# A sequence block on one core: the state-space mixer's y products two head pairs at a time, a group's sum of squares one step later

## What is computed

```python
a_cum = jnp.cumsum(a_dt, axis=-1)
xdt = x * dt[..., None]
seg = a_cum[..., :, None] - a_cum[..., None, :]
decay = jnp.exp(jnp.where(causal, seg, -jnp.inf))
cb = jnp.einsum('bclgn,bcsgn->bcgls', cm, bm)
y_diag = jnp.einsum('bcgls,bcgels,bcsgep->bclgep', cb, decay, xdt)
...
y = y + d_skip * xs
y = y.reshape(b, l, D_INNER) * jax.nn.silu(z)
y = grouped_rmsnorm(y, norm_g)
return y @ w_out
```

## Time and profile before

| what | value |
|---|---|
| median of 3 runs | 918.33 us (917.94 to 918.78) |
| profiled execution, its own time | 918.76 us |
| span in its profile | 917.0 us |
| TensorE busy | 908.1 us (99%) |
| VectorE busy | 618.6 us (67%) |
| ScalarE busy | 508.9 us (55%) |
| GpSimd busy | 37.3 us (4%) |
| chain that ended last | TensorE 96%, VectorE 2%, ScalarE 1%, DMA 1% |
| granted TensorE clock | 0.996 of full speed over the span |

### The profile page before, as it was taken

One profiled execution on the slowest core, in us unless ns is written; L12 is line 12 of the kernel. 1 busy time (PEld: TensorE's weight loads), 2 busy tenths in 40 slices (PEclk: granted clock), 3 DMA queues, 4 the chain that ended last, 5 costly groups with the idle time before them and its releaser, 6 DMA issues.

```text
span 917.0 us, 14456 instructions
## 1 busy us (share of the span) xinstructions
PE 908.1 (99%) x5920; PEld 817.0 (89%) x5920; DVE 618.6 (67%) x777; ACT 508.9 (55%) x762; POOL 37.3 (4%) x52
## 2 busy tenths in 40 slices
PE   9999999999999999999999999999999999999997
PEld 7999998888899898888888999988998898888885
DVE  7888477895764677777744846766855667777533
ACT  6565488874755574444433855666755645444333
POOL 1000011120000000000000220000000000000000
PEclk9999999999999999999999999999999999999999
DMA  9855554235552566555555697433651565555551
GB/s 283 272 183 181 161 167 133 94 106 194 184 207 92 157 209 194 195 185 183 184 186 199 224 256 238 138 139 113 212 181 46 186 205 184 185 190 189 201 197 46
DMA packets 120986, 162.27 MB, mean 177 GB/s; under 512 B 4109, under 2 KB 106965, under 8 KB 120934
## 3 DMA queue, kind: packets, MB, share of 16 engines
q1 hardware_dynamic: 117828, 151.47, 50.3%
q0 software_dynamic: 3104, 10.06, 3.5%
q10 hardware_dynamic: 2, 0.00, 0.0%
HBM read 160.45 MB, written 1.07 MB: 176 GB/s over the span
## 4 chain that ended last, share of the span: by engine, by line
PE 96%; DVE 2%; ACT 1%; DMA 1%; issue 0%; DVEq 0%
PE bank L476 25%; PE bank L548 16%; PE bank L563 9%; PE bank L554 8%; PE bank L489 8%; PE bank L496 8%; PE bank L502 8%; PE bank L628 2%; PE bank L930 2%; PE bank L901 2%; PE bank L693 1%; PE bank L820 1%; PE bank L733 1%; PE bank L1067 1%; PE bank L859 1%; PE bank L850 1%
## 5 line engine op out<-in xcount | busy, mean ns | idle before, releaser
L1501 DVE TENSOR_TENSOR w_lo<-w_raw,w_hi 128x2048 fp32r<-128x2048 f32 x134 | 306.0, 2288 | 128.9 <-ACT w_hi L1099 128.4
L1099 ACT ACTIVATE w_hi<-w_raw 128x2048 fp32r<-128x2048 f32 x134 | 256.0, 1915 | 194.3 <-DMA w_raw<-in_ffn_w_gu_dram 92.5
L548 PE MATMUL bank<-actT,w_hi 128*128 128x512 f32 x640 | 152.9, 391 | 0.0
L548 PEld LDWEIGHTS bank<-actT,w_hi 128*128 128x128 f32 x640 | 117.6, 188 | 23.0 <-issue 0.2
L554 PEld LDWEIGHTS bank<-actT,w_lo 128*128 128x128 f32 x640 | 82.1, 191 | 3.1
L554 PE MATMUL bank<-actT,w_lo 128*128 128x256 f32 x640 | 83.0, 283 | 0.0
L489 PE MATMUL bank<-actT,w_hi 128*128 128x256 f32 x560 | 74.2, 285 | 0.0
L496 PE MATMUL bank<-actT,w_hi 128*128 128x256 f32 x560 | 72.9, 283 | 0.0
L502 PE MATMUL bank<-actT,w_lo 128*128 128x256 f32 x560 | 72.9, 283 | 0.0
L489 PEld LDWEIGHTS bank<-actT,w_hi 128*128 128x128 f32 x560 | 69.6, 191 | 1.2 <-issue 0.8
L496 PEld LDWEIGHTS bank<-actT,w_hi 128*128 128x128 f32 x560 | 69.7, 192 | 0.0
(11 more groups left out here) (252 smaller groups left out, 1337.9 us busy)
## 6 DMA issues: line engine op xcount, KB each, us to landing
w_raw<-in_ffn_w_gu_dram SPq DMA_DIRECT2D x44, 1024.0 KB, 5.1
w_raw<-in_ffn_w_down_dram SPq DMA_DIRECT2D x22, 1024.0 KB, 4.9
w_raw<-in_ssm_w_in_dram SPq DMA_DIRECT2D x20, 1024.0 KB, 5.4
w_raw<-in_mem_w_kv_dram SPq DMA_DIRECT2D x16, 1024.0 KB, 5.4
w_raw<-in_ssm_w_out_dram SPq DMA_DIRECT2D x8, 1024.0 KB, 5.0
w_raw<-in_mem_w_q_dram SPq DMA_DIRECT2D x8, 1024.0 KB, 6.1
w_raw<-in_mem_w_o_dram SPq DMA_DIRECT2D x8, 1024.0 KB, 5.0
w_raw<-in_w_kv_dram SPq DMA_DIRECT2D x8, 1024.0 KB, 5.5
```

What stands on the lines that cost most here:

```text
L548: pe.matmul(bank[:, b + c, :], hi[:, slot, cols], actT[:, k].rearrange("p e n -> p (e n)"), start=k == 0, stop=False, skip_group_check=True)
L1099: act.activation(hi[:, u % SLOTS, :], raw[:, u % SLOTS, :], ACT.Copy).then_inc(w_hi_done, 1)
L1501: dve.tensor_tensor(lo[:, s, :], raw[:, s, :], hi[:, s, :].bitcast(F32), ALU.subtract).then_inc(w_lo_done, 1)
```

## The change

The y products are made for two pairs at every second step: pairs 0 and 1 in step 3, 2 and 3 in step 5, up to 14 and 15 in step 17. VectorE takes both pairs in the same step (14 and 15 still by its entry for step 16). `xtok` and `mt` get a fourth place, and ScalarE's wait for a free place looks back four pairs. The sum of squares of a group moves one step later on TensorE, and with it 1/rms, the rounded half and the remainder of the first three groups; the last group's stay. The squares on ScalarE stay where they are in each step.

```diff
--- before.py
+++ after.py
@@ -92,9 +92,11 @@
         NAME_OF.append((_name, _i))
 NUNITS = len(NAME_OF)
 
-Y_TAKEN = {p + LAG: (p,) for p in range(XT - 2)}
-Y_TAKEN[XT] = (XT - 2, XT - 1)
-Y_REST = {8: 0, 12: 1, 18: 2, 20: 3}
+Y_MADE = {p + LAG + 1: (p, p + 1) for p in range(0, XT, 2)}
+Y_TAKEN = {**Y_MADE, XT: (XT - 2, XT - 1)}
+del Y_TAKEN[XT + 1]
+Y_REST = {9: 0, 13: 1, 18: 2, 20: 3}
+RS_STEPS = {6: 0, 10: 1, 14: 2, 17: 3}
 SSD_SPLITS, SSD_COPIES = {}, {}
 for _n, (_name, _i) in enumerate(SSD_FILL_UNITS):
     _step = fill_step(6 * _n)
@@ -245,9 +247,9 @@
 
 
         conv_acc, o = shared("conv_acc", [P, 2, 2, S], F32, 0)
-        xtok, o = shared("xtok", [P, 3, ST, P], F32, 0)
+        xtok, o = shared("xtok", [P, 4, ST, P], F32, 0)
         at_mt = o
-        mt, o = shared("mt", [P, 3, 2, CAUS], F32, o)
+        mt, o = shared("mt", [P, 4, 2, CAUS], F32, o)
         first_row, _ = shared("first_row", [P, D], F32, 0)
         ones_row, _ = shared("ones_row", [P, P], F32, 4096)
         cum_rest, o1 = shared("cum_rest", [P, S], F32, at_mt + 2048)
@@ -817,9 +819,9 @@
                     pe.wait_ge(y_ready, j - 1)
                 for e in range(2):
                     rows = slice(e * HD, (e + 1) * HD)
-                    pe.matmul(bank[rows, 3 + j % 2 * 3, 0:S], xtok[:, j % 3, 0, rows], mt[:, j % 3, e, 0:S],
+                    pe.matmul(bank[rows, 3 + j % 2 * 3, 0:S], xtok[:, j % 4, 0, rows], mt[:, j % 4, e, 0:S],
                               start=True, stop=False, skip_group_check=True)
-                    ins = pe.matmul(bank[rows, 3 + j % 2 * 3, P:S], xtok[:, j % 3, 1, rows], mt[:, j % 3, e, S:CAUS],
+                    ins = pe.matmul(bank[rows, 3 + j % 2 * 3, P:S], xtok[:, j % 4, 1, rows], mt[:, j % 4, e, S:CAUS],
                                     start=False, stop=True, skip_group_check=True)
                 ins.then_inc(y_mm, 1)
 
@@ -864,13 +866,13 @@
                         ssd_cb(g + 1)
                 if j < XT:
                     fill_piece(2 * j + 1)
-                if LAG <= j < XT + LAG:
-                    ssd_y(j - LAG)
+                for pair in Y_MADE.get(j, ()):
+                    ssd_y(pair)
                 if j >= XT:
                     fill_piece(2 * j)
                     fill_piece(2 * j + 1)
-                if j > LAG + 1 and (j - LAG - 2) % GT == GT - 1:
-                    ssd_ssq((j - LAG - 2) // GT)
+                if j > LAG + 2 and (j - LAG - 3) % GT == GT - 1:
+                    ssd_ssq((j - LAG - 3) // GT)
 
             def w_out_ready(i):
 
@@ -1315,27 +1317,27 @@
                 if j < XT:
                     g = j // GT
                     act.wait_ge(xtok_mm, j + 1)
-                    act.activation(xtok[:, j % 3], bank[:, 7, 0:S].rearrange("p (t n) -> p t n", n=P), ACT.Copy).then_inc(xtok_ready, 1)
-                    if j >= 3:
-                        act.wait_ge(y_mm, j - 2)
+                    act.activation(xtok[:, j % 4], bank[:, 7, 0:S].rearrange("p (t n) -> p t n", n=P), ACT.Copy).then_inc(xtok_ready, 1)
+                    if j >= 4:
+                        act.wait_ge(y_mm, j - 3)
                     for h in (2 * j, 2 * j + 1):
 
                         act.wait_ge(row_mm, h + 1)
-                        row, decay = bank[:, 4 + h % 2, :], mt[:, j % 3, h % 2, :]
+                        row, decay = bank[:, 4 + h % 2, :], mt[:, j % 4, h % 2, :]
                         act.activation(decay[:, 0:S], row[:, 0:S], ACT.Exp, bias=dtc[:, 7, 0, h:h + 1])
                         act.activation(decay[:, S:CAUS], row[:, S:CAUS], ACT.Exp, bias=dtc[:, 7, 1, h:h + 1]).then_inc(decay_ready, 1)
                     if j % GT == CB_STEP and g + 1 < SSM_GROUPS:
                         copy_cb(g + 1)
                 if c == XT + 1:
                     hi_upto(U[("w_out", 3)])
-                if c > 1 and c % GT == 1:
-
-                    act.wait_ge(ssq_mm, c // GT)
+                if c in RS_STEPS:
+
+                    act.wait_ge(ssq_mm, RS_STEPS[c] + 1)
                     own.mark(act.activation(rs[:, 0, :], bank[:, 2, 0:S], ACT.Ln, bias=eps_col, scale=1.0 / (GT * P)))
                     own.wait()
                     act.activation(rs[:, 1, :], rs[:, 0, :], ACT.Exp, scale=-0.5).then_inc(rs_ready, 1)
-                if c > 2 and c % GT == 2:
-                    g = c // GT - 1
+                if c - 1 in RS_STEPS:
+                    g = RS_STEPS[c - 1]
                     act.wait_ge(yn_ready, g + 1)
                     act.activation(y_hi[:, g * GT:(g + 1) * GT, :], z[:, g * GT:(g + 1) * GT, :], ACT.Copy).then_inc(y_hi_done, 1)
                 if 0 < c <= XT:
@@ -1771,7 +1773,7 @@
                     if j % GT == 0:
                         dve.wait_ge(cb_causal, g + 1)
                     dve.wait_ge(decay_ready, 2 * j + 2)
-                    dve.scalar_tensor_tensor(out=mt[:, j % 3], in0=mt[:, j % 3], scalar=BIG,
+                    dve.scalar_tensor_tensor(out=mt[:, j % 4], in0=mt[:, j % 4], scalar=BIG,
                                              in1=cbT[:, g % 2:g % 2 + 1, :].broadcast_to([P, 2, CAUS]),
                                              op0=ALU.min, op1=ALU.mult).then_inc(mt_ready, 1)
                     if j % GT == CB_STEP + 1 and g + 1 < SSM_GROUPS:
@@ -1785,8 +1787,8 @@
                     dve.tensor_tensor(z[:, pair, :], z[:, pair, :], xbc[:, pair, :], ALU.mult).then_inc(y_ready, 1)
                 if c == XT + 1:
                     lo_upto(U[("w_out", 3)])
-                if c > 1 and c % GT == 1:
-                    g = c // GT - 1
+                if c in RS_STEPS:
+                    g = RS_STEPS[c]
                     dve.wait_ge(rs_ready, g + 1)
                     dve.wait_ge(y_ready, GT * (g + 1))
                     for k in range(g * GT, (g + 1) * GT):
```

## The result

The changed kernel takes **922.09 us** (median of 6 runs, 921.33 to 924.37), the kernel before, run beside it, 918.67 us (6 runs, 917.94 to 920.88). The ratio is **1.0033**, with a 95% interval of 1.0019 to 1.0047: slower by 3.4 us. The forecast was +2.7 us (921.0, range 918.9 to 922.8). The profiled execution took 922.07 us, its span is 920.3 us, against 918.76 and 917.0 before.

The account below looks back on a forecast made before the run. TensorE, busy 99%, bounds the kernel; the moved wait makes ScalarE and VectorE the bound from step 3. +2.2 up to step 15's transposes, +0.25 behind them and +0.25 queue growth give +2.7 on 918.33: 921.0 us, range 918.9 to 922.8.

Parts of the forecast that it names:

- Sign, place and mechanism: Odd steps: even pair's square waits for VectorE's product, holding up the bank 7 copy TensorE's transposes need; kernel slower.
- TensorE's own saving: Y products in eight double visits: 2.4 us from the cheaper second pair plus 0.2 from the sums, 2.6 in all.
- The start of the chain: Step 3: exponentials, then VectorE's operations on the first even pair; its square on ScalarE starts at 149.45 us.
- The loop: ScalarE and VectorE from one even square to the next, two steps each; five of them, steps 3 to 13, 39.36 us.
- From the last even square to T15: Square, cast, copy and hand-off up to the transposes of step 15: 0.30, 0.95, 0.38 and 0.1 us.
- Behind T15: After step 15's transposes: two double visits, 3.2 us, instead of three single ones, 2.85; with cheaper change-overs +0.25 us.
- the forecast's queue growth: ScalarE's operations recorded longer in a full queue: five loops of 0.05 us, +0.25.
- Moving rs, y_hi and y_lo one step costs nothing by itself: VectorE and ScalarE work after the group sums: no cost, since only the projection and the next group's sum want it.
- The saving: Rival: ScalarE keeps ahead of TensorE's transposes and the 2.6 us are gained, 915.7 us; chance 0.07.
- The shorter loop: Rival: the ScalarE and VectorE two-step loop is shorter than summed, 917.5 to 920.1 us, say 919.5; chance 0.16.
- GpSimd's additions: Rival: additions of squares slow VectorE's chain, five loops losing 0.5 us each, 923.5 us; chance 0.08.
- The second pair at its full 0.95: Rival: second pair in a TensorE visit costs a whole visit, 921.6 us; counted with the forecast, together 0.69.

Follow-up runs that it names:

- e1: Changed kernel with the squares of both pairs made together, one step behind their products: 917.65 us, ratio 0.9992 to the kernel before.
- e2: Kernel before, single visits kept, with only each even pair's square moved into the step that makes its product: 925.23 us, ratio 1.0061.
- e8: Changed kernel with squares paired one step behind their products, and the second group's y remainder in step 16 instead of 13: 917.02 us, ratio 0.998.
- e3: Changed kernel with GpSimd adding only 1 of the 256 columns of each square: 922.93 us, ratio 1.004 to the kernel before.
- e4: Kernel before with only the group sum, 1/rms, rounded half and remainder one step later, y products still single: 919.24 us, ratio 1.0004.
- e7: Changed kernel with the group sum, 1/rms, rounded half and remainder back in their old steps: 925.7 us, ratio 1.0065 to the kernel before.

## Why the prediction was right, and where it was off

- **Sign, place and mechanism were right.** The forecast was a wait of ScalarE at the even pair's square in every odd step, some 13 us in all, and behind it TensorE at its door, some 5 us over about five steps. Measured: 14.0 us, and 6.0 us in five waits (5.6 by the steps of e1). e1 takes the wait away and with it the loss; e2 makes it in the kernel before, with its loss.
- **TensorE's own saving: 2.6 forecast.** The second pair was taken at 0.65 and costs 0.69; the double visit was forecast as about 1.5 and costs 1.64. The loop of e8, in which no wait is left, gives the whole: 2.22. So the term was 0.4 too large. Eight times 2 x 0.95 - 1.64 is 2.1, not 2.4. The 0.65 came from the scores, read as 4.01 - 3.41 = 0.60; but the step of 3.41 begins behind a visit and that of 4.01 does not, so they cost 0.66. The sums give the rest, 0.1 to 0.15: a sum costs 0.49 before (two steps of 3.95 and 3.36, less twice 3.41), and 0.44 in e1 (2.96 - 2.52). Forecast were 0.2.
- **The start of the chain.** First even square at 149.45, forecast from a T0 of 136.20: 13.25 behind it. Measured 149.20 - 136.04 = 13.16.
- **The loop: 39.36 forecast, 40.35 measured. This is the term that was mis-sized.** By loops: 7.44, 7.67, 8.31, 8.14, 7.80 against 7.53, 7.79, 8.90, 8.24, 7.89. Four of them are long by 0.09 to 0.12 each. The hand-offs are not it: between the last exponential and `mt`, and between the product and the square, they are 0.03 to 0.04 each, the 0.07 of the forecast. In three of the four the last exponential is recorded longer, 0.42 to 0.44 instead of 0.38; the rest is 0.01 to 0.04 in several places. The middle one is long by 0.59. There the step said "the four products with rs 1.58"; they took 2.14, because GpSimd's addition fell on them, and e3, which makes it small, gives 0.48 of the 0.59 back. The forecast had +0.25 in place of this whole 0.99, for operations that are recorded longer in a full queue. That gave some 0.15 (0.04, 0.06 and 0.05); the largest part, 0.48, is VectorE's chain beside the addition, which the sum put at nothing.
- **From the last even square to T15:** 1.69 measured (189.55 to 191.24), 1.7 forecast.
- **Behind T15:** +0.25 forecast, +0.38 measured.
- **The sum.** +2.7 becomes 2.7 - 0.1 (start) + 1.0 (loop) - 0.25 (the forecast's queue growth, which the 1.0 has in it) + 0.1 (behind T15) = 3.45; the loop measured +3.42.
- **"Moving rs, y_hi and y_lo one step costs nothing by itself" was wrong**, by 0.6 in the kernel before (e4), behind T15. The reason given, that they are wanted late, looked at who waits for them and not at what stands behind them on VectorE. In the change itself it is hidden: it had a mere 0.38 more behind T15, since the waits ahead of it gave VectorE its time. That is argued from e4 and the table: e7 would isolate it, but its clock fell in the same stretch.
- **The rivals.** The saving did not arrive, and in the order of the queue was the reason, as said: the four places cured nothing that was ill. The shorter loop was wrong in its direction. GpSimd's additions did fall beside VectorE's work in most loops (on the products with rs again at 185.07, 2.14), but they cost time in one loop of five, where VectorE was the bound, and not on `mt`, where the rival looked for them. The second pair at its full 0.95 is excluded by the 0.69. The error of 0.4 in TensorE's own saving does not show in the result, since that saving never arrived.

## What to carry to other kernels

Where the order on each engine is written by hand, moving a producer one step later is not done until every engine's queue has been searched for a consumer that now stands in the same step; then add up what stands behind that consumer, here a cast and the copy that the bound engine needs (3.4 us lost, with no new work). Compare the length of the two-engine loop that this makes with the pace of the bound engine before the change is written: 7.5 to 8.9 against 7.0 us for two steps (e1, T3 to T13: 35.01 for five times two). And when the consumer has been moved along, look at once at who is late next: half of the saving was in moving one remainder on VectorE out of its crowded stretch (e8).

## What the runs showed of the hardware that was not expected

**VectorE slows beside a GpSimd addition.** Four products of 128x256 with rs: 1.67 alone, 2.14 beside an addition of 0.85 us; `mt` 0.94 to 0.96, and 1.49; a remainder of 128x1024 1.22, and 1.75. The price is near 0.5 us for an addition during which VectorE has no gap, and e3, with additions of one column, takes it away. It can also fall on GpSimd: the addition at 152.47 of the changed kernel took 1.27 beside an `mt` of unchanged 0.96, and the 7.52 us of e8 lie beside remainders of unchanged length (1.21 for 128x1024). Which of the two pays, and why, was not tried.

**TensorE's clock fell in e7 in a stretch with short waits.** TensorE's timeline of e7 behind T15:

```profile
193.49 0.44 PE L852 MATMUL bank<-const,xbc 128*128 128x128 f32 x2 [1.82 <-ACT xtok L1320]
193.68 1.25 PE L565 MATMUL bank<-w_hi,memT_hi 128*128 128x256 f32 x8
...
195.15 2.16 PE L565 MATMUL bank<-w_hi,memT_lo 128*128 128x256 f32 x8
```

and the windows of e7 (stretch, length, busy time of each engine, granted clock, DMA share, GB/s):

```profile
194.00:194.50 0.50, 0.50 (x7) 0.50 (x6) 0.42 (x1) 0.50 (x3) 0.00 (x0) 1.00 1.01 418
194.50:195.00 0.50, 0.50 (x5) 0.35 (x4) 0.29 (x1) 0.50 (x3) 0.00 (x0) 0.68 1.03 426
195.00:196.00 1.00, 1.00 (x5) 0.92 (x4) 1.00 (x2) 1.00 (x4) 0.88 (x1) 0.50 0.91 373
...
197.00:198.00 1.00, 1.00 (x6) 0.56 (x7) 1.00 (x2) 0.00 (x0) 0.00 (x0) 0.50 0.00 0
198.00:199.00 1.00, 1.00 (x14) 0.80 (x10) 0.64 (x2) 0.00 (x0) 0.00 (x0) 0.95 0.00 0
```

The granted clock is 0.50 (1.2 GHz) for some 3.3 us, though TensorE was busy all through 194 to 199. Eight products take 2.16 instead of 1.24. T15 to y_hi is 11.70, 1.54 more than in the changed kernel, about half of the slow stretch, as half the rate would give. Ahead of it TensorE had waited 1.82 us, and 0.53 some nine microseconds earlier. But e2 waited 2.18 and 1.93 us in the same part, and its granted clock is 1.00 throughout; the changed kernel waited 1.56 at the same place, at 1.00. So the length of one wait does not decide it, and what does is open. The five runs of e7 above 925.5 have a granted clock of 0.997 over the whole span, the one at 921.28 has 0.999, so the slow stretch seems to be in most executions of e7. If the waits brought it on, which is not shown, a wait of TensorE can cost more than its own length: in e7 the half clock took 1.54 us, nearly as much as the 1.82 before it.

**The first microseconds differ between executions of the same kernel.** The same products on the first rows of the program, TensorE's timeline of the kernel before:

```profile
5.38 1.98 PE L476 MATMUL bank<-first_row,ones_row 1*128 1x512 f32 x4
7.29 1.05 PE L733 MATMUL bank<-cum 128*128 128x256 bf16 x8
```

and of e1:

```profile
5.55 3.78 PE L478 MATMUL bank<-first_row,ones_row 1*128 1x512 f32 x4
9.26 1.89 PE L735 MATMUL bank<-cum 128*128 128x256 bf16 x8
```

They take 1.9 and 1.8 times as long, near the ratio of the two clock levels, and T0 comes 2.2 us later. The granted clock in the records does not settle it: it reads 1.00 for both kernels from 5 to 7.5 us, and for e1 also from 9.5 to 11.5, where that of before is 0.50. The totals have two groups accordingly: of 24 runs of the kernel before 19 lie at 917.45 to 919.15 and 5 at 920.82 to 921.05; of 12 of e1 seven at 916.6 to 917.7 and five at 919.75 to 919.98. There are more than two levels of T0, though: over the ten traces it lies at 135.24, at 136.0 to 136.3, at 137.4 to 137.5 and at 138.4 to 138.6. That the clock is the cause is argued, not shown. The Trainium skill, "TensorE: Matmul & The Clock Gate", Part 1, says that the number of products run at the lower clock at a kernel's start varies from run to run; the two groups would fit that. For an edit worth 1 us the median of a few runs is a poor measure here, and the length of the stretch that the edit touches, taken from the trace, a better one.
